# Two transformer blocks on one core: the sparse attention on negated scores, with wide and narrow items in turn, and weights, bias row and scan copies at other places

## The reference, cut to what matters

```python
score = jnp.einsum('bths,bth->bts', jax.nn.relu(dots), w)
_, sel = lax.top_k(score, top_k)                       # 128 of 512
bias = rel_bias[t5_bucket(q_pos[None, :, None] - sel)]
logits = (jnp.einsum('bthc,btkc->bthk', qb, kv_sel) * (dc ** -0.5) + moveaxis(bias, -1, 2))
logits = jnp.where(valid[:, :, None, :], logits, -jnp.inf)
probs = jax.nn.softmax(logits, axis=-1)
return jnp.einsum('bthk,btkc->bthc', probs, kv_sel)
...
u_gate, u_val = jnp.split(causal_depthwise_conv(xn @ w_up, conv_w, conv_b), 2, axis=-1)
ffn = (gelu(u_gate) * u_val) @ w_down
...
y_dsa = od @ dsa_w_out ; (sigmoid(gates)[gla] * y_gla + sigmoid(gates)[dsa] * y_dsa) @ w_out
```

## Time and profile before

| | |
|---|---|
| median of 3 runs | 2263.02 us (2261.51 to 2263.46) |
| profiled execution | 2263.09 us, span 2261.3 us |
| busy, of the span | PE 97%, PE weight loads 84%, DVE 43%, ACT 33%, POOL 44% |
| mean granted clock of TensorE | 0.986 |
| chain that ended last | PE 78%, issue 10%, POOL 6%, DVE 5%, ACT 1% |

### The profile page before, as it was taken

One profiled execution on the slowest core, in us unless ns is written; L12 is line 12 of the kernel. 1 busy time (PEld: TensorE's weight loads), 2 busy tenths in 40 slices (PEclk: granted clock), 3 DMA queues, 4 the chain that ended last, 5 costly groups with the idle time before them and its releaser, 6 DMA issues.

```text
span 2261.3 us, 31125 instructions
## 1 busy us (share of the span) xinstructions
PE 2202.1 (97%) x12448; PEld 1890.6 (84%) x12448; DVE 979.5 (43%) x1446; ACT 739.6 (33%) x962; POOL 1002.2 (44%) x783
## 2 busy tenths in 40 slices
PE   8999999989999998999999999999999999999998
PEld 7897988989999886888888787878777888888886
DVE  5134233458888406323201619661875442221034
ACT  4133244342222214322212324551345332222143
POOL 4322212545555544545554543254430555555454
PEclk9999999999999999999999999999999999999998
DMA  4211111212222222232222321014220222222221
GB/s 159 99 66 66 57 39 38 95 74 75 93 93 93 93 93 74 93 108 96 93 93 93 101 90 59 28 69 147 75 93 1 93 93 93 96 99 102 93 102 56
DMA packets 30108, 190.72 MB, mean 84 GB/s; under 512 B 3776, under 2 KB 4288, under 8 KB 8256
## 3 DMA queue, kind: packets, MB, share of 16 engines
q1 hardware_dynamic: 25776, 182.66, 22.8%
q10 hardware_dynamic: 4240, 6.75, 1.0%
HBM read 187.13 MB, written 2.13 MB: 84 GB/s over the span
## 4 chain that ended last, share of the span: by engine, by line
PE 78%; issue 10%; POOL 6%; DVE 5%; ACT 1%; DMA 0%; POOLq 0%; SPq 0%; DVEq 0%; ACTq 0%
PE ps L1986 68%; POOL wlo L604 5%; PE ps L2478 2%; PE ps L2249 1%; PE ps L2603 1%; ACT whi L670 1%; PE ps L2685 1%; DVE sqa L1280 1%; PE ps L2658 1%; PE ps L2576 1%; PE ps L2232 0%; PE ps L2641 0%; PE ps L2289 0%; PE ps L2675 0%; DVE sd L1832 0%
## 5 line engine op out<-in xcount | busy, mean ns | idle before, releaser
L604 POOL TENSOR_TENSOR wlo<-raw,whi 128x512 fp32r<-128x512 f32 (+2 forms) x772 | 991.2, 1316 | 1236.2 <-ACT whi L670 1167.6
L670 ACT CAST whi<-raw 128x2048 fp32r<-128x2048 f32 x167 | 319.3, 1912 | 827.8 <-PE ps L1986 766.8
L1986 PE MATMUL ps<-x2hi,whi 128*128 128x512 f32 x1136 | 451.6, 397 | 8.1 <-DVE x2lo L1268 7.6
L1986 PE MATMUL ps<-x2hi,wlo 128*128 128x512 f32 x1136 | 443.6, 391 | 0.0
L1986 PE MATMUL ps<-x2lo,whi 128*128 128x512 f32 x1136 | 443.5, 390 | 0.0
L1986 PE MATMUL ps<-xhi,whi 128*128 128x256 f32 x1344 | 278.8, 289 | 24.3 <-DVE xlo L1333 9.5
L1986 PE MATMUL ps<-xlo,whi 128*128 128x256 f32 x1344 | 275.1, 286 | 0.0
L1986 PE MATMUL ps<-xhi,wlo 128*128 128x256 f32 x1344 | 274.9, 286 | 0.0
L1986 PEld LDWEIGHTS ps<-x2hi,whi 128*128 128x128 f32 x1136 | 214.3, 189 | 58.0 <-issue 13.9
L1986 PEld LDWEIGHTS ps<-x2lo,whi 128*128 128x128 f32 x1136 | 214.4, 189 | 45.0 <-issue 2.4
L1986 PEld LDWEIGHTS ps<-x2hi,wlo 128*128 128x128 f32 x1136 | 214.1, 188 | 45.2
(11 more groups left out here) (395 smaller groups left out, 2785.3 us busy)
## 6 DMA issues: line engine op xcount, KB each, us to landing
raw<-wstream SPq DMA_DIRECT2D x170, 1024.0 KB, 4.8
h<-h SPq DMA_DIRECT2D x4, 528.0 KB, 8.7
ncb<-c_rows ACTq DMA_DIRECT2D x8, 256.0 KB, 3.6
bias<-bias_rows ACTq DMA_DIRECT2D x8, 256.0 KB, 4.5
out_dram<-outb SPq DMA_DIRECT2D x4, 512.0 KB, 3.5
raw<-wstream ACTq DMA_DIRECT2D x4, 256.0 KB, 7.4
pin<-p ACTq DMA_DIRECT2D x1, 512.0 KB, 3.3
ncb<-c_rows ACTq DMA_DIRECT2D x8, 33.0 KB, 2.1
```

The lines of the kernel that those rows point to most:

```text
L604: return nc.gpsimd.tensor_tensor(wlo[b][:, cols], raw[b][:, cols], whi[b][:, cols].bitcast(F32), ALU.subtract)
L670: nc.scalar.copy(whi[b][:], raw[b][:]).then_inc(sig("hi_done"), 1)
L1986: ins = mm(dst, w[slot][:, cols], xx(tok), start=first and p_ == 0, stop=last and p_ == 2, skip_group_check=True)
```

## The change

Eight edits, by place:

1. Up projection: ACT's list becomes cast of `U_UP + 4`, gelu 0, cast of `U_UP + 5`, hidden cast 0; cast of `U_UP + 6`, gelu 1, hidden cast 1; cast of `U_UP + 7`, gelu 2, hidden cast 2; the loop starts at pair 3.
2. Bias row: products go into the bank pair of unit `U_GQK` (free after three evacuations); PE no longer waits for the copy before the first half of GV, only before the second half. The copy negates.
3. Scan copies: `ckvt` and `iwt` are written before the fourth scan.
4. Negated scores: `dq`, the bias row and the masks carry the opposite sign, so the bias instruction takes a minimum, which is the exp's bias as it is; the negating instruction and the wait before it go. The exp gets scale -1. A negated causal mask for block 0 is written to `mj` ahead of the indexer.
5. The items go in pairs for each head: blocks 3 and 0 for the 8 heads, then blocks 2 and 1.
6. The high and low part of an output are taken one step later (n - 4), and ACT's high part stands first in its step.
7. ACT: the table for exp is loaded ahead of the wait for the masks; the last side tile is copied, with its sigmoid after the loop.
8. The cast of `U_DSAO + 1` moves from step 1 to four quarters in steps 8 to 11, its low part is made in 16 pieces of 128 columns. The first unit of `U_DSAO` waits for every second low part.

```diff
-        DI = [(j, hd) for j in range(4) for hd in range(8)]
+        DI = [(j, hd) for js in ((3, 0), (2, 1)) for hd in range(8) for j in js]
...
-        PIECE = {u: P for u in (U_UP, U_UP + 1, U_F1I, U_F1I + 1, U_GR + 3, U_MG1)}
+        PIECE = {u: P for u in (U_UP, U_UP + 1, U_F1I, U_F1I + 1, U_GR + 3, U_MG1, U_DSAO + 1)}
...
 (ACT)
-            for i in range(2):
-                hi_of(U_UP + 4 + i)
+            for i in range(3):
+                hi_of(U_UP + (4, 6, 7)[i])
                 act.wait_ge(sig("gate_ready"), i + 1)
                 if i:
                     act.wait_ge(sig("prod"), i)
                 conv_gate(i)
+                if i == 0:
+                    hi_of(U_UP + 5)
                 act.wait_ge(sig("prod"), i + 1)
                 nc.scalar.copy(hhi[:, 2 * i:2 * i + 2, :], cvl[:]).then_inc(sig("hid_hi"), 1)
-            with act.Fori(2, FC // 2) as i:
+            with act.Fori(3, FC // 2) as i:
...
-                    side_out(U_DQ, c, dq[:, c, :], bank(4 + c % 4), ACT.Copy, float(np.float32(P ** -0.5)))
+                    side_out(U_DQ, c, dq[:, c, :], bank(4 + c % 4), ACT.Copy, -float(np.float32(P ** -0.5)))
+                elif c == 15:
+                    side_out(U_DQ, c, g2[:, c - 8, :], bank(4 + c % 4), ACT.Copy, cast=False)
...
-            act.wait_ge(sig("mask_ready"), 3)
-            for n in range(ND + 3):
+            nc.scalar.preload_act_table_set("natural_log_exp_and_others")
+            act.wait_ge(sig("mask_ready"), 4)
+            for n in range(ND + 4):
+                m = n - 4
+                if 0 <= m < ND:
+                    j, hd = DI[m]
+                    act.wait_ge(sig("da_o"), m + 1)
+                    nc.scalar.copy(x2hi[:, hd, j * P:(j + 1) * P], bank(6 + m % 2)[:, 0:P]).then_inc(sig("da_hi"), 1)
                 m = n - 2
...
-                    nc.scalar.activation(dl[n % 3][:, 0:w], dl[n % 3][:, 0:w], ACT.Exp, bias=dst_[:, 0, n:n + 1],
-                                         accum_out=dst_[:, 1, n:n + 1]).then_inc(sig("da_exp"), 1)
+                    nc.scalar.activation(dl[n % 3][:, 0:w], dl[n % 3][:, 0:w], ACT.Exp, scale=-1.0,
+                                         bias=dst_[:, 0, n:n + 1], accum_out=dst_[:, 1, n:n + 1]
+                                         ).then_inc(sig("da_exp"), 1)
                 if n == 1:
                     beside_indexer(15)
-                m = n - 3
-                if 0 <= m < ND:
-                    j, hd = DI[m]
-                    act.wait_ge(sig("da_o"), m + 1)
-                    nc.scalar.copy(x2hi[:, hd, j * P:(j + 1) * P], bank(6 + m % 2)[:, 0:P]).then_inc(sig("da_hi"), 1)
+                if 8 <= n < 12:
+                    hi_quarter(U_DSAO + 1, n - 8)
+            act.wait_ge(sig("evac2"), U_DSAO - U_GQK)
+            nc.scalar.activation(g2[:, 7, :], g2[:, 7, :], ACT.Sigmoid).then_inc(sig("squashed"), 1)
 (DVE)
-            vec.tensor_copy(brow[:], ps[0:8, 4 * BANK:4 * BANK + 640]).then_inc(sig("brow_ready"), 1)
+            at_ = 2 * (U_GQK % 2) * BANK
+            vec.tensor_scalar(brow[:], ps[0:8, at_:at_ + 640], -1.0, None, ALU.mult).then_inc(sig("brow_ready"), 1)
...
             for hd in range(4):
+                if hd == 3:
+                    dve.wait_ge(sig("ckv_turned"), 1)
+                    step.up(vec.tensor_copy(ckvt[:].rearrange("p j c -> p (j c)"), bank(4)))
+                    vec.tensor_scalar(iwt, bank(0)[:, 0:32], float(np.float32(8 ** -0.5)), None, ALU.mult
+                                      ).then_inc(sig("iw_ready"), 1)
                 step.up(vec.tensor_tensor_scan(nbt[:, hd, :], restart[:], ax[:, hd, :], 0.0, ALU.mult, ALU.add))
...
+            vec.tensor_scalar(mj[:, 0:P], madd.bitcast(F32), -1.0, None, ALU.mult).then_inc(sig("mask_ready"), 1)
...
-                    step.up(vec.tensor_tensor_reduce(dl[n % 3][:, 0:w], bank(n % 4)[:, 0:w],
-                                                     bias[:, hd, w - 1::-1], 1.0, -3e38, ALU.add, ALU.max,
-                                                     dst_[:, 2, n:n + 1]))
-                    step.wait()
-                    vec.tensor_scalar(dst_[:, 0, n:n + 1], dst_[:, 2, n:n + 1], -1.0, None, ALU.mult
-                                      ).then_inc(sig("da_max"), 1)
+                    vec.tensor_tensor_reduce(dl[n % 3][:, 0:w], bank(n % 4)[:, 0:w], bias[:, hd, w - 1::-1], 1.0, 3e38,
+                                             ALU.add, ALU.min, dst_[:, 0, n:n + 1]).then_inc(sig("da_max"), 1)
...
-                m = n - 3
+                m = n - 4
                 if 0 <= m < ND:
                     j, hd = DI[m]
                     dve.wait_ge(sig("da_hi"), m + 1)
...
+                if c == 3:
+                    dve.wait_ge(sig("squashed"), 2)
 (PE)
-            mm(bank(4)[0:8], relb[:], bucket[:, 0:BANK], start=True, stop=True)
-            mm(bank(5)[0:8, 0:P], relb[:], bucket[:, BANK:BANK + P], start=True, stop=True
+            pe.wait_ge(sig("evac2"), 3)
+            mm(bank(2 * (U_GQK % 2))[0:8], relb[:], bucket[:, 0:BANK], start=True, stop=True)
+            mm(bank(2 * (U_GQK % 2) + 1)[0:8, 0:P], relb[:], bucket[:, BANK:BANK + P], start=True, stop=True
                ).then_inc(sig("brow_done"), 1)
-            pe.wait_ge(sig("brow_ready"), 1)
...
                 if half and first:
                     pe.wait_ge(sig("evac2"), 4)
+                    pe.wait_ge(sig("brow_ready"), 1)
...
-            units(U_DSAO, 4, x2hi, x2lo, ND - KC, "da_lo")
+            units(U_DSAO, 4, x2hi, x2lo, ND - 2 * KC + 1, "da_lo", 2)
```

More of the change, by code:

```diff
@@ L1118, in _ @@
             act.wait_ge(sig("evac2"), U_MG1 + 2 - U_GQK)
-            nc.scalar.activation(g1s[:], g1s[:], ACT.Sigmoid).then_inc(sig("g1s_on"), 1)
+            nc.scalar.activation(g1s[:], g1s[:], ACT.Sigmoid).then_inc(sig("squashed"), 1)
             for u in range(U_MG1 + 2, U_DQ):
@@ L1777, in _ @@
                               ).then_inc(sig("nb_ready"), 1)
-            dve.wait_ge(sig("ckv_turned"), 1)
-            step.up(vec.tensor_copy(ckvt[:].rearrange("p j c -> p (j c)"), bank(4)))
-            vec.tensor_scalar(iwt, bank(0)[:, 0:32], float(np.float32(8 ** -0.5)), None, ALU.mult
-                              ).then_inc(sig("iw_ready"), 1)
             def halves(ap, L):
@@ L1858, in _ @@
                 if c == 0:
-                    dve.wait_ge(sig("g1s_on"), 1)
+                    dve.wait_ge(sig("squashed"), 1)
                 vec.tensor_tensor(g1[:, rows], (g1s if c < 2 else g1)[:, rows], pair(bank(2 * glao_at(c), 2)), ALU.mult
@@ L1873, in _ @@
                     if m:
-                        dve.wait_ge(sig("mask_ready"), m // 8)
+                        dve.wait_ge(sig("mask_ready"), m // 8 + 1)
                     vec.tensor_scalar(a, rl[m % 7][:, 0:w], wcol, None, ALU.mult).then_inc(sig("ix_acc"), 1)
@@ L1889, in _ @@
                         step.wait()
-                    vec.tensor_scalar(mj[:, mj_at[j]:mj_at[j] + w], a, -2e38, NEG, ALU.is_gt, ALU.mult
+                    vec.tensor_scalar(mj[:, mj_at[j]:mj_at[j] + w], a, -2e38, -NEG, ALU.is_gt, ALU.mult
                                       ).then_inc(sig("mask_ready"), 1)
-            dve.wait_ge(sig("mask_ready"), 3)
+            dve.wait_ge(sig("mask_ready"), 4)
             dve.wait_ge(sig("bias_in"), 128)
-            for n in range(ND + 3):
+            for n in range(ND + 4):
                 if n < ND:
@@ L1994, in places_of, with unit @@
                 return [(bank(2 * b + c), slice(0, SEQ))]
-            def unit(b, T, xh, xl, x_base=None, chunks=2, x_sig="x_ready", to=None, sums=None):
+            def unit(b, T, xh, xl, x_base=None, chunks=2, x_sig="x_ready", to=None, sums=None, x_step=1):
                 order = [(c, k) for c in range(chunks) for k in range(KC)]
@@ L2004, in unit @@
                     if x_base is not None and c == 0:
-                        pe.wait_ge(sig(x_sig), x_base + k + 1)
+                        pe.wait_ge(sig(x_sig), x_base + x_step * k + 1)
                     ins = tile_products(b, 2 * k + c, places_of(b if to is None else to, c, T),
@@ L2438, in _, with units @@
             swiglu(U_F1I, 1, late_second)
-            def units(u0, n, xh, xl, x_base=None, x_sig="x_ready"):
+            def units(u0, n, xh, xl, x_base=None, x_sig="x_ready", x_step=1):
                 def one(b, i, wait_out, base=None):
@@ L2446, in one @@
                         pe.wait_ge(sig("evac2"), i + (u0 - 1 - U_GQK))
-                    unit(b, SEQ, xh, xl, base, x_sig=x_sig)
+                    unit(b, SEQ, xh, xl, base, x_sig=x_sig, x_step=x_step)
                 peel = 2 if x_base is not None else 0
@@ L2653, in _ @@
                     if j:
-                        pe.wait_ge(sig("mask_ready"), j)
+                        pe.wait_ge(sig("mask_ready"), 5 - j)
+                    else:
+                        pe.wait_ge(sig("mask_ready"), 1)
                     if n >= 4:
@@ L2658, in _ @@
```

(3 more changed lines are left out.)

## The result

| | before | changed |
|---|---|---|
| first comparison, 4 and 4 runs | 2262.27 us (2259.43 to 2263.46) | 2244.59 us (2243.03 to 2246.93) |
| second, 11 and 6 runs | 2259.69 (2257.73 to 2264.93) | 2245.20 (2242.55 to 2246.81) |
| third, 9 and 5 runs | 2260.10 (2258.57 to 2263.54) | 2246.01 (2242.54 to 2246.69) |
| profiled execution | 2263.09, span 2261.3 | 2243.3, span 2241.5 |

The ratio is 0.9925 (0.9907 to 0.9942) in the first, 0.9935 (0.9923 to 0.9947) and 0.9927 (0.9913 to 0.9940) in the others: faster by 17.7, 14.5 and 14.1 us. The forecast was 12.7 us faster, and its range ended at 2245.5, 0.9 us above the measured time. The direction was right, the size too small.

What follows compares the result with a forecast made beforehand. PE, busy 97% of the span, was taken to bound, so gains come from its idle, half clock or own work. Terms 5.2 + 2.8 - 0.8 + 5.5 = 12.7 off 2263.1 gave 2250.4 us, range 2245.5 to 2255.5.

Steps and rivals of the forecast that it cites:

- A: Sparse attention: PE binds in all 16 pairs, attention gains 10, total gain 17.2, time 2245.9 us; chance 0.2.
- the mis-sized term: Up projection: earlier casts remove PE's 4.42 us wait, about 0.5 more and 1.7 of half clock; gain 5.2 us.
- so 1.7 is given back: Up projection: low part of `U_UP + 8` ready at 586.3, PE wants it at 584.5, so PE waits about 1.7 us.
- the 6.9 that the prediction gave as its upper bound: Up projection: gain of 6.9 us from the removed waits and half clock, before anything is given back at `U_UP + 8`.
- the lower bound: Up projection: gain of only 2.0 us, with 3 us given back at `U_UP + 8` and its clock stretch.
- The idle 1.1: Bias row: PE's 1.1 us idle between the row's last product and GV goes, as only GV's second half needs the copy.
- The 1.7 of clock: Bias row: the half-clock stretch after PE's idle piece goes too, 1.7 us more, making 2.8.
- DVE's sum of work before it is the same: Start of GLA: DVE's work before the factor PE awaits is unchanged, so earlier scan copies gain 0 by themselves.
- The half-clock stretch put at -0.8: Start of GLA: PE's idle in one 3.1 us piece may cost a half-clock stretch, up to 1.7; taken as -0.8.
- Start and pair periods: Sparse attention: 7.9 us to the end of the third scores, pairs of 3.74 (blocks 3, 0) and 3.18 (2, 1).
- Pairs give PE 3.03 for either pair: Sparse attention: PE's own work is 3.03 us per pair, whether blocks 3 and 0 or blocks 2 and 1.
- Rival C: Sparse attention: new order saves only the start, pairs take 4.05 on DVE and ACT; gain 8.2, 2254.9 us; chance 0.1.

## Why the prediction was right in sign and short in size

By its own terms, foreseen and shown by the stages: 5.2 and 6.8, 2.8 - 0.8 and 2.7, 5.5 and 6.1; 12.7 against 15.6. No rival came true. A's time, 2245.9, is the nearest to the measured 2244.6, but by luck: its mechanism, an attention of 57 us with PE binding in every pair, isn't there (60.7 us, pairs of 3.70).

- **Up projection, the mis-sized term.** The step "so 1.7 is given back" failed. It took 6.80 for every four convolution steps beside POOL and 6.5 for POOL, the prices of a lot in which all four steps are held. In the changed kernel the first lot took 6.88, but the second began 0.06 us ahead of POOL and took 5.84, and the low part of `U_UP + 8` took 5.85. In the changed kernel's clock, 2.9 earlier, the prediction had that low part ready at 583.4; it was ready at 581.0: 1.0 from the second lot, 0.65 from POOL, the rest from some tenths along the chain. PE in turn came 0.6 earlier than foreseen. A wait forecast as the small difference of long sums (586.3 against 584.5) hung on which engine would start first. Without it the term is the 6.9 that the prediction gave as its upper bound (its parts, 4.42 + 0.5 + 0.2 + 1.7, make 6.8, and the lower bound, 6.9 - 3 - 1.7, makes 2.2 and not 2.0); 6.8 was measured. This is more than half of the 2.9 us by which the stages exceed the sum.
- **Bias row.** The idle 1.1 was right. The 1.7 of clock was read from one trace as a consequence of the wait; three traces with the same wait have none, and with the edit there is always a stretch at the thin products. A longer stretch there costs 0.4 to 1.0: with 6.8 us of it the way from the row to GLA's second item took 88.0 to 88.5 us, with 3.4 us 87.5 to 87.6, as PE waits for DVE's factor at its end in either case. So 1.7 of the 2.8 failed. The idle 1.1 and the 0.7 of the scans make 1.8 of the 2.7 measured; the rest lies in where stretches of half clock fell, and is luck as far as the runs show.
- **Scan copies.** "DVE's sum of work before it is the same" failed: the copies now lie where a scan would have waited for its turn behind POOL, 0.7 us. In the changed kernel the fourth scan took 1.56. The half-clock stretch put at -0.8 isn't the edit's, as shown above.
- **Attention.** Start and pair periods were right to 0.1 us, the total to 0.8. What failed beside the size is the reasoning that the order saves anything: "Pairs give PE 3.03 for either pair" was compared with a kernel that still had the old cycle in its narrow steps. With edits 4 and 6 and items by blocks, the last four steps of block 0 take 0.91 on average, block 1's 1.28, block 2's 1.72 and block 3's 2.42 (PE's own work). That is 3.3 for one of 3 and one of 0, where the pair takes 3.70, and 3.0 for 2 and 1, where it takes 3.14; and the first four narrow items are hidden beside the side tiles, where with pairs two of the four are wide. Rival C was near this (pairs save little beyond the start) but had the pair at 4.05. Beside POOL's moved low part two wide norms took 0.69 and 0.79 instead of 0.49, and two pairs 3.81 and 3.92 instead of 3.70, 0.3 in all, as in the sum. By the rule of the Trainium skill (SBUF — State Buffer, Who interferes with whom) it would have been nearer 1. The trace agrees with the rule, that the second to come waits until the first ends: the norm ends 0.28 or 0.29 us after a piece of POOL's. But few norms in the chain met a piece, and these two took 0.20 and 0.30 longer. The first of them, behind POOL's piece:

```profile
1687.57 0.46 POOL L604 TENSOR_TENSOR wlo<-raw,whi 128x128 fp32r<-128x128 f32 x1
1687.63 0.69 DVE L1923 TENSOR_SCALAR dl<-dl,dst 128x512 f32<-128x512 f32 x1
```

- **The range.** 2263.1 - 15.6 is 2247.5, inside it. Part of the miss is that 3 runs of before stood for a kernel whose medians were 2259.7 to 2261.0 in four later comparisons: from 2260.1, the sum of the stages gives 2244.5, and 2244.6 was measured. So of the 5.8 us between forecast and measured time 2.9 are the terms above, and the rest is the starting point. The range had no term for the clock in untouched code, which alone moves a trace by 5 us.

What stays open: why identical thin work is at 1.2 GHz for 6.8 us in one execution and for 17.0 in another, and what sets where the stretch between bias row and GLA falls: behind the row, at the thin products or at GLA's start. No run separated these.

## What to carry to other kernels

Cut two traces at the same instructions before explaining a difference, and begin with the code that nobody touched; here it held 2.9 of 19.8 us. Price an edit against the kernel that has its neighbours' edits too: a new order that relieves a cycle is worth nothing once the cycle itself is shortened, and may bring a longer one. Where two engines hold each other up, look at single instructions: a sum taken from a lot in which every one was held misleads by a whole turn, 1.0 us here. When side work is put into a pipeline, put it in steps that the target engine doesn't bind; the same four casts, moved with their low part, cost 2.4 us less in the other place.

## What the runs showed of the hardware

- The same instructions took 482.9 to 488.1 us in 18 traces, in steps of 1.6, one for each 3.4 us at 1.2 GHz.
- An idle wait of 0.90 us on PE behind thin products was followed by half clock in one trace of four.
- On 128x512, a convolution step of DVE took 0.74 us with POOL idle and 1.78 when it started during a subtraction piece of POOL's; a scan 1.22 when it started ahead of a piece and up to 2.25 during one; a wide norm 0.49 and 0.69. The held ones ended 0.55, 1.08 and 0.28 us after POOL's piece. A piece of POOL's took 1.29 alone and 1.74 in turn with such steps.
- A copy out of PSUM (128x512) took 0.66 on DVE during POOL's pieces and 0.69 without.
- An exp started 0.01 us after the table load of 1.28 us ahead of it ended.
